# A two-block transformer kernel on one Trainium2 core: the last blocks of rows turned on VectorE and moved by DMA, not turned by TensorE

## The chip, the cores and the metric

The kernel runs on one core of one Trainium2 chip, in one launch. The metric is device time in microseconds (us) of that core. The engines are TensorE (PE, and PEld for its weight loads), VectorE (DVE), ScalarE (ACT), GpSimd (POOL) and SyncE (SP); all but VectorE and TensorE also issue DMAs. A trailing q (SPq, POOLq) is an engine's sequencer.

## The reference

One transformer block of each of two kinds, over 256 rows of width 2048, all in float32. Cut to the matrix products that matter:

```python
# first block
h = rmsnorm(x, attn_norm_g);  proj = h @ w_in          # c_q, c_kv, k_rope, u_pool, gates
q = (rmsnorm(c_q, q_a_norm_g) @ w_q_b);  kv = (rmsnorm(c_kv, kv_a_norm_g) @ w_kv_b)
y_attn = causal_block_attention(q, k, v) @ w_attn_o;   y_pool = pooled @ w_pool_o
mixed = g_pool * y_pool + g_attn * y_attn
x = x + mixed @ w_out
h2 = rmsnorm(x, ffn_norm_g)
x = x + (silu(h2 @ w_ffn_gate) * (h2 @ w_ffn_up)) @ w_ffn_down      # D_FF 5632
# second block
h = rms_norm(x, g_mix);  proj = h @ w_in_2             # q, k, v, u, v_sg, gates
merged = sigmoid(gate_a) * (o @ w_oa) + sigmoid(gate_b) * (s @ w_ob)
x = x + merged @ w_out_2
h2 = rms_norm(x, g_ff);  x = x + square(relu(h2 @ w_ff1)) @ w_ff2   # D_FF_2 8192
```

`o` is a stick-breaking attention and `s` a spatial gating unit. Each product's left operand has to stand in SBUF with its 2048 columns on the partitions, that is, turned.

## The kernel before, in words

**Products.** Each float32 product is three products of a reduced float32 kind: the left operand is kept as `lhs_hi` and its remainder `lhs_lo` (for 4 to 8 chunks of 128: `low_hi`, `low_lo`), each weight as `w_hi` and `w_lo`. SyncE loads 1 MB of weights at a time into `raw` (four slots), ScalarE copies them to `w_hi` (`hi`, L592), VectorE subtracts to get `w_lo` (`lo`, L1109). The unit is a granule: two chunks of 128 reduction rows by 512 output columns, for 256 rows of x, so twelve products (L1803, L1806, L1810). A panel is 512 output columns; a full one has eight granules in four groups. In ffn_last, panels 2 to 9 are short, with two granules each. The copies run four granules ahead of TensorE, and the loads three to four groups ahead (SyncE waits for `lo_ready`).

**Stages.** The stages follow in the order of `PLAN`: in, pool, heads_first, heads, heads_last, attn_o, out, ffn_first, ffn (nine turns of a loop), ffn_last, in2, gates2, mix2, out2, ffn2_first, ffn2 (fourteen turns), ffn2_last.

**Stage changes.** Between two stages the rows that a stage leaves (in `mix`, or in `xres` times a gain) become the left operand of the next, in four blocks of 512 columns. Each block can be written as soon as TensorE is done with that part of the old operand, and TensorE waits for it (`lhs_ready`) ahead of the group that reads it. There are two ways to turn a block:
- on TensorE: `pieces` transposes it in eight parts of 128x128 into PSUM (L1831, tile `aux`), ScalarE copies them to `lhs_hi` (L624), VectorE subtracts to get `lhs_lo` (L1146);
- in squares: VectorE turns all 32x32 squares in place (`flip_rows`, L1163) into `turn_x`, GpSimd issues sixteen DMAs of 32 KB that put the squares in their places in `turn_t` (`move_rows`, L551), ScalarE copies (`moved_block`, L657) and VectorE subtracts (`moved_block`, L1170). There are two buffers, so block n waits for block n - 2.

At attn_o to out, out to ffn_first, mix2 to out2 and out2 to ffn2_first (the four inner changes; functions `bridge`) the first three blocks go in squares and the fourth by TensorE, in the middle of the next stage's first panel (`gemm_after`, behind its second group). The fourth can only be started when the old stage's last panel is done. At ffn_last to in2 all four blocks go by TensorE. The two blocks of the low-rank rows (`cq_rows`, `ckv_rows`) are turned by TensorE in heads_first (`turn_low`, sixteen transposes).

**What sets the order.** Every engine's program is written out by hand, and each engine runs its own in order. Engines wait on semaphores; an instruction that waits holds up all behind it on its engine. GpSimd's and SyncE's DMAs are issued in their program's order too.

Of the kernel before, what the change touches and what calls it, by code (L numbers as in the profile page):

```python
# [38 lines left out]
P = 128  # L39
TOK = 2  # L40
# [127 lines left out]
def two_blocks(nc, x, positions, attn_norm_g, w_in, b_gate, q_a_norm_g, w_q_b, kv_a_norm_g, w_kv_b,  # L168
# [151 lines left out]
    rows_ready = sem("rows_ready")  # L320
# [7 lines left out]
    low_rows = sem("low_rows")  # L328
    low_turned = sem("low_turned")
# [26 lines left out]
    row_moved = [sem(f"row_moved{i}") for i in range(2)]  # L356
    flipped = sem("flipped")
# [31 lines left out]
    with block:  # L389

        @block.sync
        def _(sp):
# [11 lines left out]

            w1, w2 = w_in[0], w_in_2[0]
# [39 lines left out]
            for p in range(4):  # L445
                load(At("out"), p, w_out[0], p * N)
            at = At("ffn_first")
            load(at, 0, w_ffn_gate[0], 0)
            load(at, 1, w_ffn_up[0], 0)
# [14 lines left out]
            for p in range(10):  # L464
                load(At("in2"), p, w2, starts[p // 2] + p % 2 * N)
# [11 lines left out]
            for p in range(4):  # L477
                load(At("out2"), p, w_out_2[0], p * N)
# [25 lines left out]
        def _(pool):  # L504
# [20 lines left out]
            pool.wait_ge(low_turned, 4)  # L525
# [17 lines left out]
            def move_rows(n):  # L543
# [12 lines left out]
            for n in range(6):  # L556
                move_rows(n)
# [5 lines left out]
            with pool.Fori(1, NB1) as b:  # L563
                move(b)
            pool.wait_ge(side_go, 3)
# [9 lines left out]
            for n in range(6, 12):  # L575
                move_rows(n)
# [5 lines left out]
        def _(act):  # L582
# [172 lines left out]
            def turned_low():  # L755

                for q in range(4):
                    act.wait_ge(low_turned, q + 1)
                    c0, t = 4 * (q // 2), q % 2
                    nc.scalar.activation(low_hi[:, c0:c0 + 4, t * P:(t + 1) * P],  # L760
                                         aux[:, q, :].rearrange("p (c t) -> p c t", c=4),
                                         ACT.Copy).then_inc(low_hi_ready, 1)
# [54 lines left out]
            def sub(at, p, u, has_last, last=False):  # L817
# [5 lines left out]
                if has_last:  # L823
                    attend_b(u)
                else:
                    turned_low()
# [97 lines left out]
            hi(at, 6, 4, 8)  # L924
            squares_of(0, at, 6)
            pieces(3, 0)
            hi(at, 6, 8, 10)
            squares_of(1, at, 7)
            pieces(3, 1)
            hi(at, 6, 10, 12)  # L930
            squares_of(2, at, 8)
            pieces(3, 2)
            hi(nxt, 0, 4, 6)
            squares_of(3, at, 9)
            pieces(3, 3)
            hi(nxt, 0, 6, 8)
# [162 lines left out]
        def _(dve):  # L1099
# [34 lines left out]
            def gained(b):  # L1134
# [3 lines left out]
                                gain[:, c].unsqueeze(1).broadcast_to([P, TOK, N]), ALU.mult  # L1138
                                ).then_inc(rows_ready, 2)

            def pieces(n_hi, kq):

                for p in (2 * kq, 2 * kq + 1):
                    dst = slice(p % 2 * P, (p % 2 + 1) * P)
                    dve.wait_ge(lhs_hi_ready, n_hi + p + 1)
                    v.tensor_tensor(lhs_lo[:, 4 * kq:4 * kq + 4, dst],  # L1146
                                    aux[:, p % 4, :].rearrange("p (c t) -> p c t", c=4),
                                    lhs_hi[:, 4 * kq:4 * kq + 4, dst].bitcast(F32),
                                    ALU.subtract).then_inc(lhs_ready, 1)
# [23 lines left out]
            def bridge(n_hi, n, at, p, nxt, last_rows, between=None):  # L1173
# [10 lines left out]
                lo(nxt, 0, 4, 6)  # L1184
                pieces(n_hi, 3)
                lo(nxt, 0, 6, 8)
# [82 lines left out]
            dve.sem_inc(rows_ready, 8)  # L1269
# [53 lines left out]
            dve.sem_inc(low_rows, 1)  # L1323
# [10 lines left out]
            def turned_low():  # L1334
                for q in range(4):
                    dve.wait_ge(low_hi_ready, 8 + q + 1)
                    c0, t = 4 * (q // 2), q % 2
# [896 lines left out]
```

## Time and profile before

| | us |
|---|---|
| median of 3 runs | 2652.7 (2651.62 to 2652.74) |
| profiled execution | 2651.66 |
| its span, first to last instruction | 2650.0 |
| TensorE busy, 11949 products | 2643.5 |
| VectorE busy | 1662.7 |
| ScalarE busy | 1311.6 |
| GpSimd busy | 379.0 |

TensorE is busy all the time, so its row is the schedule: what is put on it lengthens the span, and so does what it waits for. The other engines' idle time is the slack in which they keep ahead. The granted clock of TensorE was full throughout in the profile, and the DMA engines moved 200 GB/s on average. In rows in order of time, an entry is the start, the duration of the run of like instructions, engine and line, operation, output from inputs, count, and in brackets the idle time ahead with what ended it. Products overlap, so a row's duration is a little longer than the distance to the next.

### The profile page before, as it was taken

Reading aid. Unit: us, or ns where it says so; the run is one execution under the profiler, and the core shown is the slowest. Engines: PE = TensorE matmul, PEld = TensorE weight load, DVE = VectorE, ACT = ScalarE, POOL = GpSimd, SP = SyncE. Lnnn points to the kernel's source line nnn. Section 1 sums busy time; section 2 is a strip of 40 time slices with the busy share of each in tenths; the row PEclk is TensorE's granted clock in tenths of the full one; section 3 lists DMA queues with packets and bytes.
Section 4 is the critical chain, followed back from the end, with each engine's and each line's share of the span. In section 5 each row is a group of like instructions: output and inputs, shape, how many; then the busy total and the mean of one; then the engine's idle time right before and its main releaser. Section 6 shows DMA issues by size and latency. Waiting matters only on the chain.

```text
span 2650.0 us, 33467 instructions
## 1 busy us (share of the span) xinstructions
PE 2643.5 (100%) x11949; PEld 2202.1 (83%) x11949; DVE 1662.7 (63%) x1671; ACT 1311.6 (49%) x1501; POOL 379.0 (14%) x767
## 2 busy tenths in 40 slices
PE   9999999999999999999999999999999999999999
PEld 8888888888888888888888888888888888888887
DVE  6556777666565665665576645556666666666666
ACT  5446666445444444444454547774454444444443
POOL 1000000222111111101103220003222121212121
PEclk9999999999999999999999999999999999999999
DMA  8555544666665666666667665456666666666664
GB/s 278 182 185 180 174 155 162 214 213 216 223 198 199 201 203 205 199 197 201 203 214 215 207 206 175 174 191 212 209 209 207 207 210 198 206 201 211 203 208 151
DMA packets 278041, 529.96 MB, mean 200 GB/s; under 512 B 20032, under 2 KB 26608, under 8 KB 277584
## 3 DMA queue, kind: packets, MB, share of 16 engines
q1 hardware_dynamic: 251600, 493.91, 56.1%
q0 software_dynamic: 26192, 35.01, 4.9%
q8 instruction: 46, 0.75, 0.1%
q14 instruction: 27, 0.22, 0.0%
q10 hardware_dynamic: 176, 0.07, 0.0%
HBM read 502.69 MB, written 2.10 MB: 190 GB/s over the span
## 4 chain that ended last, share of the span: by engine, by line
PE 99%; DVE 1%; DVEq 0%; DMA 0%; ACT 0%; issue 0%; ACTq 0%
PE pair L1810 27%; PE pair L1803 27%; PE pair L1806 27%; PE aux L1806 4%; PE aux L1810 4%; PE aux L1803 4%; PE aux L1831 1%; PE aux L1991 0%; PE aux L1988 0%; PE pair L1892 0%; PE pair L1899 0%; PE pair L1896 0%; PE aux L1950 0%; PE aux L2006 0%; PE aux L2123 0%; DMA act_t<-in_attn_norm_g 0%
## 5 line engine op out<-in xcount | busy, mean ns | idle before, releaser
L1109 DVE TENSOR_TENSOR w_lo<-raw,w_hi 128x1024 fp32r<-128x1024 f32 x944 | 1133.7, 1211 | 816.9 <-ACT w_hi L592 807.5
L592 ACT ACTIVATE w_hi<-raw 128x1024 fp32r<-128x1024 f32 (+2 forms) x942 | 983.3, 1051 | 1188.5 <-PE pair L1810 991.7
L1803 PE MATMUL pair<-w_hi,lhs_hi 128*128 128x512 f32 x2176 | 587.5, 392 | 0.0
L1810 PE MATMUL pair<-w_lo,lhs_hi 128*128 128x512 f32 x2176 | 582.4, 390 | 0.5 <-DVE w_lo L1109 0.5
L1806 PE MATMUL pair<-w_hi,lhs_lo 128*128 128x512 f32 x2176 | 582.4, 390 | 0.0
L1810 PEld LDWEIGHTS pair<-w_lo,lhs_hi 128*128 128x128 f32 x2176 | 408.5, 188 | 86.0 <-DVE w_lo L1109 0.9
L1806 PEld LDWEIGHTS pair<-w_hi,lhs_lo 128*128 128x128 f32 x2176 | 408.6, 188 | 85.5
L1803 PEld LDWEIGHTS pair<-w_hi,lhs_hi 128*128 128x128 f32 x2176 | 405.9, 188 | 81.8
L540 POOL DMA_DIRECT2D arena<-arena x544 | 265.7, 497 | 1276.3 <-DVE arena L1522 1044.6
L1803 PE MATMUL pair<-w_hi,low_hi 128*128 128x512 f32 (+1 forms) x1048 | 278.7, 388 | 0.0
L1806 PE MATMUL pair<-w_hi,low_lo 128*128 128x512 f32 (+1 forms) x1048 | 277.2, 386 | 0.0
L1810 PE MATMUL pair<-w_lo,low_hi 128*128 128x512 f32 (+1 forms) x1048 | 276.9, 386 | 0.0
L1806 PEld LDWEIGHTS pair<-w_hi,low_lo 128*128 128x128 f32 x1048 | 196.4, 188 | 38.5
L1810 PEld LDWEIGHTS pair<-w_lo,low_hi 128*128 128x128 f32 x1048 | 196.1, 188 | 38.4
L1803 PEld LDWEIGHTS pair<-w_hi,low_hi 128*128 128x128 f32 x1048 | 195.1, 188 | 38.2
L1456 DVE TENSOR_TENSOR xres<-xres,pair 128x1024 f32<-128x1024 f32 x115 | 139.7, 1215 | 1.9 <-PE pair L1810 1.9
L1810 PE MATMUL aux<-w_lo,lhs_hi 128*128 128x512 f32 x480 | 128.4, 389 | 0.0
L1806 PE MATMUL aux<-w_hi,lhs_lo 128*128 128x512 f32 x480 | 128.4, 389 | 0.0
L1803 PE MATMUL aux<-w_hi,lhs_hi 128*128 128x512 f32 x480 | 128.4, 389 | 0.0
L551 POOL DMA_DIRECT2D arena<-arena x192 | 93.8, 497 | 213.9 <-DVE arena L1163 143.9
L1810 PEld LDWEIGHTS aux<-w_lo,lhs_hi 128*128 128x128 f32 x480 | 90.1, 188 | 18.7
L1806 PEld LDWEIGHTS aux<-w_hi,lhs_lo 128*128 128x128 f32 x480 | 90.1, 188 | 18.7
(236 smaller groups left out, 1193.2 us busy)
## 6 DMA issues: line engine op xcount, KB each, us to landing
raw<-in_w_ff SPq DMA_DIRECT2D x128, 1024.0 KB, 5.1
raw<-in_w_in SPq DMA_DIRECT2D x118, 1024.0 KB, 5.1
raw<-in_w_ffn_gate SPq DMA_DIRECT2D x44, 1024.0 KB, 5.1
raw<-in_w_ffn_up SPq DMA_DIRECT2D x44, 1024.0 KB, 5.0
raw<-in_w_ffn_down SPq DMA_DIRECT2D x44, 1024.0 KB, 5.0
raw<-in_w_out SPq DMA_DIRECT2D x32, 1024.0 KB, 5.3
arena<-arena POOLq DMA_DIRECT2D x736, 32.0 KB, 3.9
raw<-in_w_attn_o SPq DMA_DIRECT2D x16, 1024.0 KB, 5.1
```

The lines of the kernel that those rows point to most:

```text
L540: pool.dma_start(dst[f * 32:(f + 1) * 32, a], src[a * 32:(a + 1) * 32, f]).then_inc(moved, 16)
L551: pool.dma_start(turn_t[n % 2][f * 32:(f + 1) * 32, a], turn_x[n % 2][a * 32:(a + 1) * 32, f]).then_inc(row_moved[n % 2], 16)
L592: nc.scalar.activation(w_hi[:, at.slot(p, k), :, 0:width], raw[:, at.raw_slot(p, k), 2 * h:2 * h + 2, 0:width], ACT.Copy).then_inc(hi_read ...
L1109: v.tensor_tensor(w_lo[:, at.slot(p, k), :, 0:n], raw[:, at.raw_slot(p, k), 2 * h:2 * h + 2, 0:n], w_hi[:, at.slot(p, k), :, 0:n].bitcast( ...
L1456: v.tensor_tensor(xs, xs, ps, ALU.add)
L1803: nc.tensor.matmul(ps[:, t, 0:n], hi_t[:, ch, tok], w_hi[:, s, c, 0:n], start=start and k == 0 and c == 0, stop=False)
L1806: nc.tensor.matmul(ps[:, t, 0:n], lo_t[:, ch, tok], w_hi[:, s, c, 0:n], start=False, stop=False)
L1810: mm = nc.tensor.matmul(ps[:, t, 0:n], hi_t[:, ch, tok], w_lo[:, s, c, 0:n], start=False, stop=stop and 2 * k + c == kch - 1)
L1831: return nc.tensor.transpose(dst, src, ident[0:src.shape[0], :])
```

## The change

All transposes of rows by TensorE at the stage changes are taken out, and so are those of the low-rank rows.
- The fourth block of the four inner changes is turned in squares, with all sixteen moves issued by GpSimd. VectorE's turn stands behind the block's last addition or gain; the copy and the subtraction stand between the splits of granules 6 and 7 of the next stage's first panel.
- At ffn_last to in2 all four blocks go in squares, and eight of each block's sixteen moves are issued by GpSimd and eight by SyncE, between its weight loads (`HALVED`, `move_half`).
- The low-rank rows are turned at the start of the pool stage by two turns on VectorE and 32 moves from GpSimd, and copied and subtracted in heads_first.
- The semaphores follow; the blocks are numbered four to a change.

The core of the diff (on SyncE some loads of out, ffn_first and out2 are also written as two calls, which issue the same DMAs):

```diff
+    low_x = [part(0, 4, 4 * TOK, 32), part(2048, 4, 4 * TOK, 32)]
+    low_t = [part(1024, 4, 4 * TOK, 32), part(3072, 4, 4 * TOK, 32)]
-    BLOCKS = [(r, f, kq) for r, f in ((1, 2), (2, 3), (4, 6), (5, 7)) for kq in range(3)]
+    BLOCKS = [(r, f, kq) for r, f in ((1, 2), (2, 3), (3, 4), (4, 6), (5, 7)) for kq in range(4)]
+    HALVED = [r == 3 for r, f, kq in BLOCKS]
...
@@ SyncE
+            def move_half(n):
+                sp.wait_ge(row_flipped, n + 1)
+                r, f, kq = BLOCKS[n - 2]
+                sp.wait_ge(lhs_ready, 8 * f + 2 * kq + 2)
+                for f in range(2, 4):
+                    for a in range(4):
+                        sp.dma_start(turn_t[n % 2][f * 32:(f + 1) * 32, a],
+                                     turn_x[n % 2][a * 32:(a + 1) * 32, f]).then_inc(half_moved[n % 2], 16)
...
-            for p in range(10):
-                load(At("in2"), p, w2, starts[p // 2] + p % 2 * N)
+            at = At("in2")
+            load(at, 0, w2, 0, groups=[0])
+            for b in range(4):
+                load(at, (b + 1) // 4, w2, (b + 1) // 4 * N, groups=[(b + 1) % 4])
+                move_half(8 + b)
+            load(at, 1, w2, N, groups=[1, 2, 3])
...
@@ GpSimd
-            pool.wait_ge(low_turned, 4)
+            pool.wait_ge(low_flipped, 2)
+            for b in range(2):
+                for f in range(4):
+                    for a in range(4):
+                        pool.dma_start(low_t[b][f * 32:(f + 1) * 32, a], low_x[b][a * 32:(a + 1) * 32, f]
+                                       ).then_inc(low_moved, 16)
...
-                for f in range(4):
+                for f in range(2 if HALVED[n] else 4):
...
@@ ScalarE, bridge
-                hi(nxt, 0, 4, 6)
-                pieces(r, 3, at.gran(p, 8) + SPLIT)
-                hi(nxt, 0, 6, 8)
+                hi(nxt, 0, 4, 7)
+                moved_block(n + 3, 3, at.gran(p, 8) + SPLIT)
+                hi(nxt, 0, 7, 8)
...
@@ VectorE, bridge
                 last_rows()
-                lo(nxt, 0, 4, 6)
-                pieces(n_hi, 3)
-                lo(nxt, 0, 6, 8)
+                flip_rows(n + 3)
+                lo(nxt, 0, 4, 7)
+                moved_block(n_hi, n + 3, 3)
+                lo(nxt, 0, 7, 8)
...
@@ VectorE, ffn_last
             for j in range(4):
-                lo(at, 6 + j, 4, 6)
+                lo(at, 6 + j, 4, 5)
                 add_x(at, 6 + j, j * N)
                 gained(j)
-                if j:
-                    pieces(28, j - 1)
-            lo(nxt, 0, 4, 6)
-            pieces(28, 3)
-            lo(nxt, 0, 6, 8)
+                flip_rows(8 + j)
+                if j >= 2:
+                    moved_block(28, 6 + j, j - 2)
+                lo(at, 6 + j, 5, 6)
+            lo(nxt, 0, 4, 5)
+            moved_block(28, 10, 2)
+            lo(nxt, 0, 5, 7)
+            moved_block(28, 11, 3)
+            lo(nxt, 0, 7, 8)
...
@@ TensorE
-            def gemm_after(at, f, left, c0=0, r=None, ps=None):
+            def gemm_after(at, f, left, c0=0, ps=None):
                 for g in range(4):
                     pe.wait_ge(lhs_ready, 8 * f + 2 * g + 2)
                     gemm(at, 0, left, c0, [g], ps)
-                    if g == 1:
-                        pieces(r, f, 3)
...
-                else:
-                    turn_low()
...
             for j in range(4):
                 gemm(at, 6 + j, low, 4)
-                if j:
-                    pieces(3, 4, j - 1)
```

**Order at out to ffn_first, VectorE, before.** L1170 is the subtraction of a block that came in squares, L1456 the last panel's addition to `xres`, L1137 the gain, L1109 a split of weights, L1146 the subtraction of a block turned by TensorE.

```order
L1109 TENSOR_TENSOR w_lo<-raw,w_hi 128x1024 x4
L1170 TENSOR_TENSOR lhs_lo<-arena,lhs_hi 128x1024
L1456 TENSOR_TENSOR xres<-xres,pair 128x2x512
L1137 TENSOR_TENSOR mix<-xres,arena 128x2x512
L1109 TENSOR_TENSOR w_lo<-raw,w_hi 128x1024 x2
L1146 TENSOR_TENSOR lhs_lo<-aux,lhs_hi 128x4x128 x2
L1109 TENSOR_TENSOR w_lo<-raw,w_hi 128x1024 x6
```

The same place after the change, by the changed kernel's lines: L1190 is the subtraction, L1476 the addition, L1165 the gain, L1183 the turn in squares, L1137 a split of weights.

```order
L1137 TENSOR_TENSOR w_lo<-raw,w_hi 128x1024 x4
L1190 TENSOR_TENSOR lhs_lo<-arena,lhs_hi 128x1024
L1476 TENSOR_TENSOR xres<-xres,pair 128x2x512
L1165 TENSOR_TENSOR mix<-xres,arena 128x2x512
L1183 STREAM_TRANSPOSE arena<-mix 128x8x4x32
L1137 TENSOR_TENSOR w_lo<-raw,w_hi 128x1024 x3
L1190 TENSOR_TENSOR lhs_lo<-arena,lhs_hi 128x1024
L1137 TENSOR_TENSOR w_lo<-raw,w_hi 128x1024 x5
```

The turn comes in behind the gain, and the fourth block's subtraction moves from behind two splits of the next stage to behind three.

**Order at ffn_last to in2, VectorE, before**, from the addition of panel 7 on.

```order
L1456 TENSOR_TENSOR xres<-xres,pair 128x2x512
L1137 TENSOR_TENSOR mix<-xres,arena 128x2x512
L1146 TENSOR_TENSOR lhs_lo<-aux,lhs_hi 128x4x128 x2
L1109 TENSOR_TENSOR w_lo<-raw,w_hi 128x1024 x2
L1456 TENSOR_TENSOR xres<-xres,pair 128x2x512
L1137 TENSOR_TENSOR mix<-xres,arena 128x2x512
L1146 TENSOR_TENSOR lhs_lo<-aux,lhs_hi 128x4x128 x2
```

After the change, from the addition of panel 7 to the turn of panel 9.

```order
L1476 TENSOR_TENSOR xres<-xres,pair 128x2x512
L1165 TENSOR_TENSOR mix<-xres,arena 128x2x512
L1183 STREAM_TRANSPOSE arena<-mix 128x8x4x32
L1137 TENSOR_TENSOR w_lo<-raw,w_hi 128x1024 x2
L1476 TENSOR_TENSOR xres<-xres,pair 128x2x512
L1165 TENSOR_TENSOR mix<-xres,arena 128x2x512
L1183 STREAM_TRANSPOSE arena<-mix 128x8x4x32
L1190 TENSOR_TENSOR lhs_lo<-arena,lhs_hi 128x1024
L1137 TENSOR_TENSOR w_lo<-raw,w_hi 128x1024 x2
L1476 TENSOR_TENSOR xres<-xres,pair 128x2x512
L1165 TENSOR_TENSOR mix<-xres,arena 128x2x512
L1183 STREAM_TRANSPOSE arena<-mix 128x8x4x32
```

Per panel there is one turn more, and block 0's subtraction, which stood behind the gain of panel 7, now stands behind the turn of panel 8.

## Rows read from the trace of the kernel before

**Rows 1.** The page: busy engines (us, share, instructions); shares of the last chain.
```profile
PE 2643.5 (100%) x11949; PEld 2202.1 (83%) x11949; DVE 1662.7 (63%) x1671; ACT 1311.6 (49%) x1501; POOL 379.0 (14%) x767
PE 99%; DVE 1%; DVEq 0%; DMA 0%; ACT 0%; issue 0%; ACTq 0%
```

**Rows 2.** Costliest groups: busy, mean ns | idle before, its releaser.
```profile
L1109 DVE TENSOR_TENSOR w_lo<-raw,w_hi 128x1024 fp32r<-128x1024 f32 x944 | 1133.7, 1211 | 816.9 <-ACT w_hi L592 807.5
```

**Rows 3.** TensorE reading mix: ns min/median/max, first and last start.
```profile
L1831 PE MATMUL aux<-con,mix x80: 270/273/274, 172.1 to 1961.2; 128*128 128x128 f32 x80
```

**Rows 4.** Order of time, out to ffn_first: start us, us, engine, line.
```profile
638.62 1.07 PE L1803 MATMUL pair<-w_hi,lhs_hi 128*128 128x512 f32 x4
641.12 1.22 DVE L1170 TENSOR_TENSOR lhs_lo<-arena,lhs_hi 128x1024 fp32r<-128x1024 f32 x1
642.26 1.22 DVE L1456 TENSOR_TENSOR xres<-xres,pair 128x1024 f32<-128x1024 f32 x1
643.59 1.22 DVE L1137 TENSOR_TENSOR mix<-xres,arena 128x1024 f32<-128x1024 f32 x1
644.73 2.35 DVE L1109 TENSOR_TENSOR w_lo<-raw,w_hi 128x1024 fp32r<-128x1024 f32 x2
649.51 1.04 PE L1831 MATMUL aux<-con,mix 128*128 128x128 f32 x8
650.30 1.17 PE L1803 MATMUL pair<-w_hi,lhs_hi 128*128 128x512 f32 x4
```

**Rows 5.** Order of time, TensorE in heads_first.
```profile
172.08 1.91 PE L1831 MATMUL aux<-con,mix 128*128 128x128 f32 x16
173.74 1.17 PE L1803 MATMUL pair<-w_hi,lhs_hi 128*128 128x512 f32 x4
```

**Rows 6.** Order of time, the first block of stage out.
```profile
577.25 1.23 DVE L1137 TENSOR_TENSOR mix<-xres,arena 128x1024 f32<-128x1024 f32 x1 [0.19 <-issue]
578.57 1.25 DVE L1163 STREAM_TRANSPOSE arena<-mix 128x1024 f32<-128x1024 f32 x1
579.74 2.32 DVE L1109 TENSOR_TENSOR w_lo<-raw,w_hi 128x1024 fp32r<-128x1024 f32 x2
580.11 7.81 POOL L551 DMA_DIRECT2D arena<-arena  x16 [32.84 <-DVE arena L1163]
```

**Rows 7.** Order of time, moves in in2 that ScalarE waited for.
```profile
1570.39 7.81 POOL L540 DMA_DIRECT2D arena<-arena  x16 [14.15 <-DVE arena L1522]
1581.30 1.06 ACT L1006 ACTIVATE act_t<-arena 128x1024 f32<-128x1024 f32 x1 [3.04 <-DMA arena<-arena]
```

**Rows 8.** DMA issues from 1573.5, 1577.5, 609.1, 647.0: count, size, landing us.
```profile
arena<-arena POOLq DMA_DIRECT2D x2, 32.0 KB, 1.9
arena<-arena POOLq DMA_DIRECT2D x2, 32.0 KB, 3.6
arena<-arena POOLq DMA_DIRECT2D x2, 32.0 KB, 5.2
raw<-in_w_ffn_up SPq DMA_DIRECT2D x1, 1024.0 KB, 5.0
```

**Rows 9.** Windows: busy us (count) by engine, PEclk, DMA share, GB/s.
```profile
649.00:651.40 2.40, 2.40 (x16) 2.06 (x16) 0.62 (x2) 1.25 (x3) 0.00 (x0) 1.00 0.98 370
651.60:654.60 3.00, 3.00 (x15) 2.47 (x14) 2.83 (x3) 2.86 (x6) 0.00 (x0) 1.00 0.00 1
```

**Rows 10.** Order of time, attn_o to out.
```profile
550.69 1.07 PE L1803 MATMUL pair<-w_hi,lhs_hi 128*128 128x512 f32 x4
557.00 2.36 DVE L1109 TENSOR_TENSOR w_lo<-raw,w_hi 128x1024 fp32r<-128x1024 f32 x2
```

**Rows 11.** Order of time, TensorE at ffn_last, panel 7.
```profile
1341.31 1.07 PE L1803 MATMUL pair<-w_hi,low_hi 128*128 128x512 f32 x4
```

**Rows 12.** Filler products at the start, and window 0 to 3 us.
```profile
L1873 PE MATMUL pair<-arena x30: 275/276/581, 1.2 to 8.3; 128*128 128x128 f32 x30
0.00:3.00 3.00, 1.80 (x8) 1.81 (x9) 0.71 (x3) 1.12 (x1) 0.20 (x4) 1.00 0.33 69
```

More of the change, by code:

```diff
@@ L356, in two_blocks @@
     row_moved = [sem(f"row_moved{i}") for i in range(2)]
+    half_moved = [sem(f"half_moved{i}") for i in range(2)]
     flipped = sem("flipped")
@@ L444, in _ @@
                 load(at, 2 + p, w_attn_o[0], p * N)
-            for p in range(4):
-                load(At("out"), p, w_out[0], p * N)
+            at = At("out")
+            load(at, 0, w_out[0], 0)
+            load(at, 1, w_out[0], N, groups=[0])
+            load(at, 1, w_out[0], N, groups=[1, 2, 3])
+            for p in range(2, 4):
+                load(at, p, w_out[0], p * N)
             at = At("ffn_first")
             load(at, 0, w_ffn_gate[0], 0)
-            load(at, 1, w_ffn_up[0], 0)
+            load(at, 1, w_ffn_up[0], 0, groups=[0])
+            load(at, 1, w_ffn_up[0], 0, groups=[1, 2, 3])
             def ffn_block(at, i):
@@ L463, in _ @@
             starts = (0, SB, COL_VS, COL_U, 2 * SB)
-            for p in range(10):
-                load(At("in2"), p, w2, starts[p // 2] + p % 2 * N)
+            at = At("in2")
[4 more added lines that the diff above has]
+            load(at, 1, w2, N, groups=[1, 2, 3])
+            for p in range(2, 10):
+                load(at, p, w2, starts[p // 2] + p % 2 * N)
             with sp.Fori(0, 2) as i:
@@ L476, in _ @@
                 load(At("mix2", i), 1, w_oa_2[0], i * N)
-            for p in range(4):
-                load(At("out2"), p, w_out_2[0], p * N)
+            at = At("out2")
+            load(at, 0, w_out_2[0], 0)
+            load(at, 1, w_out_2[0], N, groups=[0])
+            load(at, 1, w_out_2[0], N, groups=[1, 2, 3])
+            for p in range(2, 4):
+                load(at, p, w_out_2[0], p * N)
             load(At("ffn2_first"), 0, w_ff1_2[0], 0)
@@ L555, in _ @@
             to_all(gain, ffn_norm_g[0], "gain")
-            for n in range(6):
+            for n in range(8):
                 move_rows(n)
@@ L564, in _ @@
                 move(b)
+            for n in range(8, 12):
+                move_rows(n)
             pool.wait_ge(side_go, 3)
@@ L574, in _ @@
             to_all(gain, g_ff_2[0], "gain")
-            for n in range(6, 12):
+            for n in range(12, 20):
                 move_rows(n)
@@ L752, in _, with moved_low @@
                     hi(at, p, 4, 8)
[L755 to L762, printed above, removed]
+            def moved_low():
+                act.wait_ge(low_moved, 512)
+                for b in range(2):
+                    nc.scalar.activation(hid_rows(low_hi, 4 * b), low_t[b].rearrange("p a n i -> p n a i"),
+                                         ACT.Copy).then_inc(low_hi_ready, 2)
             def attend_a(u):
@@ L1137, in gained @@
                 v.tensor_tensor(mix[:, :, c], xres[:, :, c],
[L1138 to L1149, printed above, removed]
+                                gain[:, c].unsqueeze(1).broadcast_to([P, TOK, N]), ALU.mult)
+                dve.drain()
             def refill(n_hi, kq):
@@ L1322, in _ @@
             low_norm(4, 2, 2, gain_ckv, ckv_rows)
-            dve.sem_inc(low_rows, 1)
+            for b, rows in enumerate((cq_rows, ckv_rows)):
+                v.transpose(low_x[b].rearrange("p f n i -> p n f i"),
+                            rows.rearrange("p t (c d) -> p c t d", c=4)).then_inc(low_flipped, 1)
             with dve.Fori(0, 2) as i:
@@ L1508, in out_panels @@
                 bridge(n_hi, n, at, 3, nxt, last_block)
-            out_panels(At("out"), At("ffn_first"), 20, 3, 1)
+            out_panels(At("out"), At("ffn_first"), 20, 4, 1)
             def hid_turn(b, c0=0):
@@ L1959, in _ @@
                         gemm(At("pool", i), p, low, groups=[g])
-            def turn_low():
-                pe.wait_ge(low_rows, 1)
-                for q in range(4):
-                    rows = cq_rows if q < 2 else ckv_rows
-                    for c in range(4):
-                        ins = turn(aux[:, q, c * P:(c + 1) * P], rows[:, q % 2, c * P:(c + 1) * P])
-                    ins.then_inc(low_turned, 1)
             def turn_qk(u):
```

100 lines of the change are left out of this document (42 added, 58 removed).

## The prediction

> **What bounds the kernel now.** I read the busy times first, then the chain that ended last, then the waits, then the order of time at each place where one weight stage hands over to the next. TensorE is busy for 2643.5 of 2650.0 us and makes up 99% of the chain [rows 1]. The splitting of weights on VectorE, 1133.7 us, is the largest other group, and it waits for ScalarE and TensorE, not they for it [rows 2]. So two things change the time: TensorE instructions that go, and waits put in front of TensorE.
>
> One granule (twelve products of 512 columns) takes 2.72 us: from 638.62, the start of ffn_first, to 649.51 there are four, 10.89 us [rows 4]. A whole panel is eight of them, 21.76 us, one of the short panels of ffn_last two, 5.44 us.
>
> **What is removed.** 80 turns by TensorE go: the whole group that reads mix [rows 3]. Sixteen stand in heads_first, eight at each of the four inner changes (attn_o to out, out to ffn_first, mix2 to out2, out2 to ffn2_first), 32 between ffn_last and in2. Eight cost 650.30 - 649.51 = 0.79 us, and the four products behind them last 1.17 in place of 1.07 us: 0.89 in all [rows 4]. Sixteen cost 173.74 - 172.08 = 1.66, and the same 0.10 behind them: 1.76 [rows 5]. The sum is 8 x 0.89 + 1.76 = 8.9 us off TensorE, if nothing waits.
>
> **heads_first.** The two squares of the low-rank rows are turned at the start of the pool stage. VectorE gets two turns of 1.25 us there and GpSimd 32 moves of 7.81 / 16 = 0.49 us, 15.6 us [rows 6]. Between that and the use lie four panels of four granules and more, 43.5 us. I take no wait; GpSimd's memset and bias load behind them have the same slack. Gain 1.76.
>
> **The four inner changes.** This is the step that decides. In before, the fourth block was added, multiplied and turned on TensorE with time to spare. Now it goes through VectorE's turn, sixteen moves from GpSimd's queue, ScalarE's copy and VectorE's subtraction, and TensorE wants it at the fourth group of the next stage's first panel, six granules in: E + 16.32, where E is the start of that stage. At out to ffn_first, E = 638.62:
> - VectorE subtracts the third block from 641.12, adds the residual at 642.26, multiplies by the gain at 643.59, and goes on at 644.73, E + 6.1 [rows 4]. An earlier block shows the turn 1.32 us behind the gain, with the drain: E + 6.29. It lasts 1.25, and GpSimd starts 0.29 behind its end (580.11 against 578.57 + 1.25): E + 7.83 [rows 6].
> - Sixteen issues take 7.81 us, so the last starts 7.32 in: E + 15.15. This is the term that eats the time: the last square isn't asked for until 1.2 us before TensorE wants the whole block.
> - Landing of the last. With the DMA engines free, issues land in 1.9 us; while a 1 MB weight load runs, 3.6 and 5.2 us [rows 8]. In before a load issued at 647.0 to 647.5 lands after 5.0, and the engines carry 0.98 of their capacity from 649.0 to 651.4 and nothing from 651.6 to 654.6 [rows 8, 9]. It is released by VectorE's split of granule 5, which now comes one turn later, so the load's packets are through near 653.1. The last move is issued at 653.8, behind a small backlog. I take 2.2, next to the 1.9 of free engines: E + 17.35.
> - ScalarE's copy 1.06 [rows 7], about 0.2 to VectorE's start, subtraction 1.22 [rows 4], 0.1 to TensorE: E + 19.95.
>
> TensorE waits 19.95 - 16.32 = 3.6 us. Bounds: landing 1.9 gives 3.3, landing 5.2 gives 6.6. The only move in before that a reader waited for was read 10.91 us behind its first issue (1570.39 to 1581.30) against my 7.32 + 2.2 = 9.5; that gives 5.0 [rows 7]. There a load ran to the end, so I keep 3.6.
>
> The other three changes have the same distances; attn_o to out has E = 550.69, and VectorE is free for the turn at 557.00, E + 6.31 [rows 10]. Four waits: 14.4 us. Queued behind the waiting copy and subtraction are the split of granule 7 and of the next panel's first granules; ScalarE needs about 1.1 us for each (its copies of that size, rows 7) and VectorE 1.21 [rows 2], where TensorE takes 2.72, and granule 7 is wanted only 2.72 us after the wait ends, so nothing more is late. The gain is 4 x 0.89 = 3.6, the net +10.8.
>
> By the Trainium skill, page "DMA: Bandwidth & Descriptors", section "Anatomy of one DMA — SWDGE (gpsimd) path", a GpSimd DMA costs a fixed 2.0 us or so plus its bytes over about 436 GB/s; an estimate from that page is 2.1 us for 32 KB, and the sum would be 0.4 us lower over the four changes. This trace agrees on free engines and not under a load, where it shows 5.2.
>
> **ffn_last to in2.** All four blocks go by squares, eight moves on GpSimd and eight on SP, while short panels of 5.44 us run. GpSimd needs 3.9 us a block, so issue isn't the limit; VectorE is. From start to start of the next it takes per panel two splits (1.15 us each), the addition (1.33), the gain (1.32), the turn (1.17) and later a subtraction (1.14): about 7.3 us against 5.44 [rows 4, 6]. Panel 7 starts at 1341.31 [rows 11], and panel 6 can be added from 1341.6. From there I stack VectorE's instructions in the new order: block 0 is subtracted at about 1358.9, and in2 could start at 1341.31 + 3 x 5.44 = 1357.6. Wait 1.3. Block 1 is subtracted 7.3 later, TensorE wants it 5.44 later: 1.8 more. Block 2 follows in time (1370 against 1371.6), block 3 with about 1 us to spare. Waits 3.1 against 4 x 0.89 = 3.6 gained: net -0.5. Bounds: 0 if the stacking is loose by that much, 7 if each of blocks 2 and 3 lands as late as 5.2. SP's weight loads queue behind its moves, held up to the turn of each block; they are issued three to four groups ahead, some 16 us, and are held 3 us.
>
> **The sum.** -8.9 + 14.4 + 3.1 = +8.6 us. The profiled execution took 2651.66 us around its span of 2650.0, so 2660.3 like for like. The median of the runs shown is 1.0 higher, so 2661.3 is forecast.
>
> **Rivals.**
> - *The landing is slow after all.* Each last move lands in 3.6 us, as in the one move that was waited for [rows 7, 8]. Waits of 5.0: +5.6, 2666.9. At 5.2 with the queue in its way, 6.6 each: 2673. For it: it is the only wait for moves that these rows show. Against it: the idle stretch of rows 9. Chance 0.18.
> - *The clock falls.* At the very start the filler products last up to 581 ns where the median is 276: half speed, 1.2 for 2.4 GHz, though the profile's granted clock reads 1.00 there [rows 12]. TensorE had done nothing before. If each wait of 3.6 us ends in such a stretch of about the first product group's length, 14 products at up to twice their time, some 1.6 us are lost at each of four: 2667.7. Against it: in before TensorE never rests that long, so no row shows it. The Trainium skill, page "TensorE: Matmul & The Clock Gate", Part 1, says that the slow state is the default and that an idle TensorE returns to it. Chance 0.10.
> - *Blocks 2 and 3 are late at in2*, because GpSimd waits for the subtraction of the block two before: up to 2 us each, 2665. Chance 0.07.
> - *Faster.* The squares arrive before TensorE wants them, and only the 8.9 us less the 3.1 stay: 2646.9. The four waits would have to fall under (8.9 - 3.1) / 4 = 1.45 each for the kernel not to be slower; that is a chain 2.2 us shorter than I stack it. The rows leave no slack of that size: the sixteen issues alone fill all but 1.2 us. Chance 0.05 to the full, and 0.03 for a result between.
> - The forecast itself: 0.57.
>
> What a measurement of this kernel can tell from no change is about 0.2%, 5.3 us: 2647.4 to 2658.0. The forecast lies 3.3 above that; in one of ten of its cases the waits are short enough to fall inside. With the cases between that makes 0.09 for the same; faster keeps 0.05; slower 0.86. The range holds the forecast's own bounds (3.3 us a wait and no wait at in2, 2657) with the slow landing and the clock above: 2656 to 2672.
>
> **What would show it.** Right: at each inner change TensorE stands 3 to 5 us between the second granule of the third group and the fourth group, ended by VectorE's subtraction of lhs_lo, with ScalarE's copy ended by a DMA; about 1.3 and 1.8 us at the start of in2 and its second group, ended by VectorE without idle time ahead of it; no wait in heads_first; no turns of mix by TensorE. Wrong: ScalarE's copy starts without a wait for the moves; a gap at another granule; long products behind a gap; VectorE idle before the subtraction of block 0 in in2.

## The result and the profile after

| | before | after |
|---|---|---|
| median | 2652.16 (4 runs, 2651.56 to 2652.74) | 2674.85 (4 runs, 2673.51 to 2676.58) |
| profiled execution | 2651.66 | 2673.51 |
| its span | 2650.0 | 2671.8 |

The ratio is 1.0086, interval [1.0074, 1.0098]. The changed kernel is slower by 22.7 us. The forecast was 2661.3, within 2656 to 2672: the sign was right, the size was not. (It was built on the median of three runs of before, 2652.7; with the fourth it is 2652.16.) Like for like, the profiled executions differ by +21.85 us where the sum said +8.6.

The page of the changed kernel, busy engines and the shares of the chain that ended last, to set beside [rows 1]:

```profile
PE 2645.2 (99%) x11869; PEld 2199.6 (82%) x11869; DVE 1672.0 (63%) x1671; ACT 1311.3 (49%) x1491; POOL 441.6 (17%) x895
PE 94%; DVE 2%; POOL 1%; DMA 1%; DVEq 1%; ACT 1%; issue 1%; ACTq 0%; POOLq 0%
```

Eighty TensorE instructions are gone, and yet TensorE is busy for 1.7 us more. Fewer instructions in more busy time: some of them must have become slower. And the chain now leaves TensorE for VectorE, GpSimd and the DMAs.

The waits of TensorE, and of ScalarE from attn_o to ffn_first, in the changed kernel (for what: us in total, times, longest):

```profile
PE pair L1825 <- DVE lhs_lo L1190: 20.3, 6, 4.6
PE pair L1825 <- DVE low_lo L1533: 0.8, 1, 0.8
ACT lhs_hi L685 <- DMA arena<-arena: 17.8, 2, 9.1
```

Six waits for a block's subtraction: the four inner changes and two at in2. In the changed kernel L1825, L1828 and L1832 are the three products of a granule (L1803, L1806 and L1810 before), L1190 is the subtraction, L1183 the turn, L685 ScalarE's copy of a moved block, L590 the moves.

Order of time at attn_o to out, from E = 549.63, which answers to [rows 4] and [rows 10]:

```profile
549.63 1.07 PE L1825 MATMUL pair<-w_hi,lhs_hi 128*128 128x512 f32 x4
555.90 1.25 DVE L1183 STREAM_TRANSPOSE arena<-mix 128x1024 f32<-128x1024 f32 x1
557.43 7.82 POOL L590 DMA_DIRECT2D arena<-arena  x16 [11.44 <-DVE arena L1183]
568.23 1.06 ACT L685 ACTIVATE lhs_hi<-arena 128x1024 fp32r<-128x1024 f32 x1 [9.12 <-DMA arena<-arena]
569.38 1.23 DVE L1190 TENSOR_TENSOR lhs_lo<-arena,lhs_hi 128x1024 fp32r<-128x1024 f32 x1 [8.87 <-ACT lhs_hi L685]
570.67 2.08 PE L1825 MATMUL pair<-w_hi,lhs_hi 128*128 128x512 f32 x4 [4.56 <-DVE lhs_lo L1190]
572.54 1.91 PE L1828 MATMUL pair<-w_hi,lhs_lo 128*128 128x512 f32 x4
574.24 1.85 PE L1832 MATMUL pair<-w_lo,lhs_hi 128*128 128x512 f32 x4
575.93 1.09 PE L1825 MATMUL pair<-w_hi,lhs_hi 128*128 128x512 f32 x4
```

The turn starts at E + 6.27 and the moves at E + 7.80; the forecast had 6.29 and 7.83. From there it is off twice. ScalarE's copy starts at E + 18.60 instead of 17.35, so TensorE starts its fourth group at E + 21.04, 4.7 us late instead of 3.6. And the first twelve products behind the wait take 5.26 us from start to start (575.93 - 570.67) where a granule took 2.72 [rows 4]: 2.5 us more.

The windows around it, changed kernel (busy us and count of PE, PEld, DVE, ACT, POOL; granted clock; DMA share; GB/s), to set beside [rows 9]:

```profile
560.00:566.00 6.00, 6.00 (x27) 4.71 (x26) 0.52 (x1) 0.00 (x0) 5.25 (x11) 1.00 0.84 244
566.00:568.00 2.00, 0.11 (x1) 0.00 (x0) 0.00 (x0) 0.00 (x0) 0.00 (x0) 1.00 0.01 1
570.00:576.00 6.00, 5.33 (x13) 4.24 (x14) 4.01 (x4) 2.12 (x3) 0.00 (x0) 0.51 0.50 164
576.00:580.00 4.00, 4.00 (x19) 3.29 (x18) 1.23 (x1) 2.11 (x2) 0.00 (x0) 1.00 0.74 278
```

The granted clock reads 0.51 from 570 to 576, that is 1.2 of 2.4 GHz, and 1.00 from 576 on. What TensorE did before it fell: nothing, for 4.56 us. The first row is the other miss: while the moves are issued, the DMA engines are at 0.84 of their capacity, not free. By queue (q1 is SyncE's load, q0 are GpSimd's moves; packets, MB, share of the 16 engines), from 563 to 564 and from 564 to 565:

```profile
q1 hardware_dynamic: 192, 0.39, 100.0%
q0 software_dynamic: 12, 0.02, 4.4%
```

```profile
q0 software_dynamic: 214, 0.23, 101.2%
q1 hardware_dynamic: 23, 0.02, 7.0%
```

The load has the engines nearly to itself until 564, and the moves issued beside it get 4%. Then they are all carried at once, and the last move, issued at 564.75, comes behind them.

At the other three changes the same picture stands. The rows of the changed kernel at out to ffn_first, mix2 to out2 and out2 to ffn2_first:

```profile
664.60 2.07 PE L1825 MATMUL pair<-w_hi,lhs_hi 128*128 128x512 f32 x4 [4.15 <-DVE lhs_lo L1190]
666.47 1.82 PE L1828 MATMUL pair<-w_hi,lhs_lo 128*128 128x512 f32 x4
668.12 1.09 PE L1832 MATMUL pair<-w_lo,lhs_hi 128*128 128x512 f32 x4
...
1892.67 1.48 PE L1825 MATMUL pair<-w_hi,lhs_hi 128*128 128x512 f32 x4 [4.34 <-DVE lhs_lo L1190]
1893.95 1.91 PE L1828 MATMUL pair<-w_hi,lhs_lo 128*128 128x512 f32 x4
...
1986.11 2.08 PE L1825 MATMUL pair<-w_hi,lhs_hi 128*128 128x512 f32 x4 [4.46 <-DVE lhs_lo L1190]
1987.98 1.57 PE L1828 MATMUL pair<-w_hi,lhs_lo 128*128 128x512 f32 x4
```

Waits: 4.56 + 4.15 + 4.34 + 4.46 = 17.5 us; counted against E + 16.32 the fourth groups start 4.7, 4.3, 4.5 and 4.6 late, 18.1 in all. Slow products (what each four take beyond 0.907 us from start to start, until the pace is back): 2.6 + 1.7 + 1.8 + 1.5 = 7.6 us. (The expectations below have 7.5 for it.)

At in2 the changed kernel's TensorE waits nearly as forecast, 1.3 and 1.5 us, and the products behind keep their pace within 0.2 us, as they did behind the turns in before [rows 4]:

```profile
1369.57 1.21 PE L1825 MATMUL pair<-w_hi,lhs_hi 128*128 128x512 f32 x4 [1.30 <-DVE lhs_lo L1190]
1376.81 1.20 PE L1825 MATMUL pair<-w_hi,lhs_hi 128*128 128x512 f32 x4 [1.47 <-DVE lhs_lo L1190]
```

### The profile page after: what moved, and what is told of

It is laid out like the page before. It is cut to its first block, busy times and chain, and to the rows that moved or that the text cites. A ratio compares the mean times of both kernels' runs of the same rounds, so it can differ in the third digit from the quotient of the medians.

```text
span 2671.8 us, 33485 instructions
## 1 busy us (share of the span) xinstructions
PE 2645.2 (99%) x11869; PEld 2199.6 (82%) x11869; DVE 1672.0 (63%) x1671; ACT 1311.3 (49%) x1491; POOL 441.6 (17%) x895
## 4 chain that ended last, share of the span: by engine, by line
PE 94%; DVE 2%; POOL 1%; DMA 1%; DVEq 1%; ACT 1%; issue 1%; ACTq 0%; POOLq 0%
PE pair L1825 26%; PE pair L1828 26%; PE pair L1832 26%; PE aux L1825 4%; PE aux L1832 4%; PE aux L1828 4%; POOL arena L590 1%; PE aux L1853 1%; DMA arena<-arena 1%; DVE w_lo L1137 0%; PE aux L1989 0%; PE aux L1986 0%; DVE lhs_lo L1190 0%; DVE arena L1183 0%; PE pair L1900 0%
## 5 line engine op out<-in xcount | busy, mean ns | idle before, releaser
L1137 DVE TENSOR_TENSOR w_lo<-raw,w_hi 128x1024 fp32r<-128x1024 f32 x944 | 1132.0, 1210 | 807.2 <-ACT w_hi L633 800.2
L1825 PE MATMUL pair<-w_hi,lhs_hi 128*128 128x512 f32 x2176 | 590.2, 393 | 20.3 <-DVE lhs_lo L1190 20.3
L1828 PE MATMUL pair<-w_hi,lhs_lo 128*128 128x512 f32 x2176 | 585.0, 391 | 0.0
L1832 PE MATMUL pair<-w_lo,lhs_hi 128*128 128x512 f32 x2176 | 583.4, 390 | 0.5 <-DVE w_lo L1137 0.5
L1825 PEld LDWEIGHTS pair<-w_hi,lhs_hi 128*128 128x128 f32 x2176 | 407.5, 189 | 105.4 <-DVE lhs_lo L1190 22.8
L1828 PEld LDWEIGHTS pair<-w_hi,lhs_lo 128*128 128x128 f32 x2176 | 410.7, 189 | 86.4
L1832 PEld LDWEIGHTS pair<-w_lo,lhs_hi 128*128 128x128 f32 x2176 | 409.7, 188 | 86.6 <-DVE w_lo L1137 0.9
L579 POOL DMA_DIRECT2D arena<-arena x544 | 265.7, 497 | 1259.1 <-DVE arena L1540 1046.5
L1825 PE MATMUL pair<-w_hi,low_hi 128*128 128x512 f32 (+1 forms) x1048 | 278.5, 387 | 0.8 <-DVE low_lo L1533 0.8
L1828 PE MATMUL pair<-w_hi,low_lo 128*128 128x512 f32 (+1 forms) x1048 | 277.0, 386 | 0.0
L1832 PE MATMUL pair<-w_lo,low_hi 128*128 128x512 f32 (+1 forms) x1048 | 276.7, 386 | 0.0
L1828 PEld LDWEIGHTS pair<-w_hi,low_lo 128*128 128x128 f32 x1048 | 196.4, 188 | 38.5
L1832 PEld LDWEIGHTS pair<-w_lo,low_hi 128*128 128x128 f32 x1048 | 196.0, 188 | 38.4
L1825 PEld LDWEIGHTS pair<-w_hi,low_hi 128*128 128x128 f32 x1048 | 195.1, 188 | 39.5 <-issue 1.2
L590 POOL DMA_DIRECT2D arena<-arena x288 | 140.7, 497 | 260.4 <-DVE arena L1183 183.5
L1476 DVE TENSOR_TENSOR xres<-xres,pair 128x1024 f32<-128x1024 f32 x115 | 139.5, 1213 | 2.2 <-PE pair L1832 2.2
L1825 PE MATMUL aux<-w_hi,lhs_hi 128*128 128x512 f32 x480 | 128.3, 389 | 0.0
L1828 PE MATMUL aux<-w_hi,lhs_lo 128*128 128x512 f32 x480 | 128.3, 389 | 0.0
L1832 PE MATMUL aux<-w_lo,lhs_hi 128*128 128x512 f32 x480 | 128.3, 389 | 0.0
L1825 PEld LDWEIGHTS aux<-w_hi,lhs_hi 128*128 128x128 f32 x480 | 90.1, 188 | 18.7
L1828 PEld LDWEIGHTS aux<-w_hi,lhs_lo 128*128 128x128 f32 x480 | 90.1, 188 | 18.7
```

The lines of the kernel that those rows point to most:

```text
L579: pool.dma_start(dst[f * 32:(f + 1) * 32, a], src[a * 32:(a + 1) * 32, f]).then_inc(moved, 16)
L590: pool.dma_start(turn_t[n % 2][f * 32:(f + 1) * 32, a], turn_x[n % 2][a * 32:(a + 1) * 32, f]).then_inc(row_moved[n % 2], 16)
L1137: v.tensor_tensor(w_lo[:, at.slot(p, k), :, 0:n], raw[:, at.raw_slot(p, k), 2 * h:2 * h + 2, 0:n], w_hi[:, at.slot(p, k), :, 0:n].bitcast( ...
L1476: v.tensor_tensor(xs, xs, ps, ALU.add)
L1825: nc.tensor.matmul(ps[:, t, 0:n], hi_t[:, ch, tok], w_hi[:, s, c, 0:n], start=start and k == 0 and c == 0, stop=False)
L1828: nc.tensor.matmul(ps[:, t, 0:n], lo_t[:, ch, tok], w_hi[:, s, c, 0:n], start=False, stop=False)
```

## The experiments

All are the changed kernel with one thing altered, in two of them with two. Times are medians; each ratio is to the kernel before on the same chip. Sums over the four inner changes are of TensorE's waits in the profile and of slow products, as above; the kernel before has 0 and, behind its turns, 0.4.

| version | median us | ratio, interval | waits | slow |
|---|---|---|---|---|
| changed kernel | 2674.85 | 1.0086 [1.0074, 1.0098] | 17.5 | 7.6 |
| fourth blocks back on TensorE | 2650.51 | 0.9993 [0.9983, 1.0003] | 0 | 0.4 |
| 36 fillers in each wait | 2680.71 | 1.0110 [1.0093, 1.0127] | 0 | 0.4 |
| 18 fillers | 2667.05 | 1.0058 [1.0041, 1.0074] | 1.5 | 0.5 |
| load held back | 2665.83 | 1.0052 [1.0035, 1.0069] | 11.8 | 6.7 |
| load held back, 12 fillers | 2661.77 | 1.0037 [1.0022, 1.0051] | 1.4 | 0.6 |
| moves on two queues | 2648.23 | 0.9984 [0.9975, 0.9994] | 0.6 | 0.8 |
| the same, VectorE reordered at in2 | 2647.16 | 0.9981 [0.9972, 0.9991] | 0.4 | 0.8 |

### The fourth blocks back on TensorE

The four inner changes are as in before; heads_first and in2 stay changed.

```diff
-BLOCKS = [(r, f, kq) for r, f in ((1, 2), (2, 3), (3, 4), (4, 6), (5, 7)) for kq in range(4)]
+BLOCKS = [(r, f, kq) for r, f in ((1, 2), (2, 3), (3, 4), (4, 6), (5, 7)) for kq in range(4 if r == 3 else 3)]
... (ScalarE's copy and VectorE's subtraction back to before's; blocks numbered anew)
@@ TensorE, gemm_after, behind the second group
+    pe.wait_ge(rows_ready, last + 1)
+    for t in range(TOK):
+        for c in range(4):
+            ins = turn(aux[:, 2 + t, c * P:(c + 1) * P], mix[:, t, (12 + c) * P:(13 + c) * P])
+        ins.then_inc(turned, 1)
```

> The changed kernel with the fourth block of the four inner changes turned by TensorE again; in2 and the low-rank rows stay as changed. My theory (the loss sits in the waits at the four inner changes, 18.1 us, and in the slow products behind them, 7.5 us): all of that goes, the turns come back at 4 x 0.89 = 3.6 us, and what is left is -1.8 (heads_first) and -3.6 + 3.3 at in2: 2650 us, 2 below the kernel before. Rival (the moves and SyncE's blocks at in2 cost more than the gaps there show): 2655 or more.

Measured: 2650.51 us, and no wait at any inner change. The inner changes carry all of the loss, 2674.85 - 2650.51 = 24.3 us. The rest of the change agrees with what the sum gave it: 1.76 + 3.56 gained against 3.1 waited is 2.2 us off 2652.2, so 2650.0. It is small, though: the interval of this version holds 1, so the run by itself does not tell this gain from none.

### Thirty-six fillers ahead of the fourth group

```diff
 for g in range(4):
+    if g == 3:
+        for _ in range(fill):
+            nc.tensor.matmul(aux[:, 0, 0:P], ident, ident, start=True, stop=True)
...
-            gemm_after(at, 2, wide)
+            gemm_after(at, 2, wide, fill=36)
... (and the same for the operands 3, 6 and 7)
```

> The changed kernel with 36 filler products (128x128, some 0.11 us each, 4 us in all) on TensorE ahead of the wait for the fourth block, at each inner change. Theory A (the products behind each wait are slow because TensorE's clock fell to half while it rested): the waits stay in sum, the slow products go, -7.5 us: 2667.4. Theory B (they are slow because ScalarE and VectorE then make up three granules each at once and all read the same memory): nothing changes, 2674.9, and the product group behind the wait still lasts about 2 us. The granted clock behind the wait, 0.51 in the changed kernel, reads 1.00 by A.

Measured: 2680.71 us, neither. I had priced a filler at half of what it takes. Order of time of this version at attn_o to out:

```profile
565.50 8.20 PE L1860 MATMUL aux<-con 128*128 128x128 f32 x72
573.46 1.17 PE L1825 MATMUL pair<-w_hi,lhs_hi 128*128 128x512 f32 x4
574.46 1.07 PE L1828 MATMUL pair<-w_hi,lhs_lo 128*128 128x512 f32 x4
```

Each float32 filler is two instructions in the trace; 36 of them take 8.2 us, 0.228 each, and TensorE does not wait but fills past the block's arrival. The four fillings cost 7.96 each against E + 16.32, 31.8 us, in place of 18.1 + 7.6. One thing it does show: behind 8 us of fillers the products take 1.07, at full pace. As a test of the theory it failed, since another cost came in its place, so it was run again with the right number.

### Eighteen fillers

The same edit, with 18.

> The changed kernel with 18 filler products (128 columns each, into a bank that nothing reads) on TensorE ahead of the fourth group at each of the four inner changes. The run with 36 of them showed 0.228 us for each: 18 take 4.1 us and fit inside the waits of 4.15 to 4.56 us, where 36 took 8.2 us and ran past them. Theory A (the wait is set by the arrival of the block, and the slow products behind it by TensorE's rest): the fourth group starts when it did in the changed kernel, the products behind it take full time, the profile shows waits of 0.1 to 0.5 us there, and the 7.5 us of slow products go: 2667.4. Rival B (the slow products come from something else that happens then, such as the weights' arrival or the transfers beside them): the waits are filled, the products stay slow, 2674.9.

Measured: 2667.05 us against 2667.4 by theory A. Order of time of this version at attn_o to out, and the window behind:

```profile
565.01 4.18 PE L1860 MATMUL aux<-con 128*128 128x128 f32 x36
569.22 1.20 PE L1825 MATMUL pair<-w_hi,lhs_hi 128*128 128x512 f32 x4
...
569.00:575.00 6.00, 5.96 (x27) 4.80 (x26) 4.80 (x5) 2.75 (x3) 0.00 (x0) 1.00 0.59 198
```

The fourth group still starts late, for the block comes no sooner, but the clock reads 1.00 and the products have their pace. This version takes 7.8 us less than the changed kernel, whose trace has 7.6 of slow products. So the slow products are the price of TensorE's rest and of nothing else that happens there: the weights, the moves and the copies are the same in both. (The fourth groups start 4.2, 4.3, 4.6 and 5.3 us late here, 18.4 in all for 18.1. The last is late by more than its fillers last, and a wait of 1.15 us is left there: VectorE's turn of that block starts at E + 7.2, where it starts at E + 6.3 at attn_o to out.)

### The load held back

SyncE issues the weight load that runs beside the fourth block's moves, of groups 2 and 3 of the next panel, only when those moves have landed.

```diff
-load(at, 1, w_out[0], N, groups=[1, 2, 3])
+load(at, 1, w_out[0], N, groups=[1])
+sp.wait_ge(row_moved[1], pool_moves(3))
+load(at, 1, w_out[0], N, groups=[2, 3])
```

and the same at the other three changes.

> The changed kernel with the one weight load that overlaps the fourth block's moves held on SyncE until they have landed (groups 2 and 3 of the next panel). Theory L (the last moves land after 3.2 and not 2 us because that load fills the DMA engines): last landing near 2.0, each wait 1.2 shorter, 4.8 us less, and perhaps a shorter slow stretch behind: 2668 to 2670. Theory Q (the depth of GpSimd's own queue of sixteen does it): landings stay at 3 us and the time at 2674.9. If the held load itself comes too late, a new gap some 8 granules on, and slower.

Measured: 2665.83 us, 9.0 less. Landing of the last three moves at attn_o to out, the changed kernel (issued from 564.2 to 565.0) and this version (564.7 to 565.5), with its windows:

```profile
arena<-arena POOLq DMA_DIRECT2D x3, 32.0 KB, 3.2
```

```profile
arena<-arena POOLq DMA_DIRECT2D x3, 32.0 KB, 1.7
560.00:566.00 6.00, 6.00 (x28) 4.96 (x27) 1.04 (x1) 0.00 (x0) 5.77 (x12) 1.00 0.27 70
570.00:573.00 3.00, 3.00 (x9) 2.33 (x8) 2.82 (x3) 0.93 (x1) 0.00 (x0) 0.55 0.84 276
569.47 1.41 PE L1833 MATMUL pair<-w_hi,lhs_hi 128*128 128x512 f32 x4 [2.84 <-DVE lhs_lo L1198]
570.68 1.91 PE L1836 MATMUL pair<-w_hi,lhs_lo 128*128 128x512 f32 x4
```

With the DMA engines at 0.27 and not 0.84, the last moves land in 1.7 us instead of 3.2, and the wait is 2.84 instead of 4.56. Waits: 17.5 to 11.8; slow products 7.6 to 6.7. That is 6.6 less, and with 1.2 more at the first turn of ffn2 and at the kernel's start it makes the 5.4 us between the two profiled executions (2673.51 to 2668.10); the other 3.6 of the 9.0 between the medians no trace shows, for the profiled execution was the slowest of this version's four. TensorE waits for no weights because of the held load. A rest of 2.84 to 3.26 us is followed by slow products all the same, 1.5 to 1.8 us a change, at a granted clock of 0.55 behind the first: the clock's part hardly falls with the wait.

### The load held back, and twelve fillers

Both edits, with 12 fillers (2.7 us). It takes away both things that the forecast had left out.

> The version whose second weight load of the stage is held until the moves have landed, with 12 filler products (2.7 us) in each of its four waits of 2.84 to 3.26 us. It has both causes taken away that the forecast left out: a landing beside a load, and TensorE's clock after a rest. Theory A with L: the version with the loads held, 2665.8, less its 6.7 us of slow products: 2659.1, which is within 2.5 us of the forecast. If the landing did not grow shorter through the held load but through something else, or the slow products are not TensorE's rest, it stays at 2665.8.

Measured: 2661.77 us, 2.7 more than 2659.1. Between the profiled executions it is 6.5 us, 2668.10 to 2661.61, close to the theory's 6.7; between the medians, taken on two chips, only 4.1, for the reason given above. The trace has both effects gone: waits of 0.17, 0.42, 0.62 and 0.21 us behind the fillers, and products at full pace. This is close to the kernel that the forecast had in mind, and it stands 0.5 us from the 2661.3 forecast. That it comes so near is partly luck: its fourth groups start 3.0 to 3.5 us late, 12.8 in all for 14.4, since the last moves land in 1.7 and not 2.2, and what the sum lacks elsewhere (the last terms of the new sum below) makes up for it.

### The moves on two queues

SyncE issues eight of the sixteen moves at the inner changes too, as at in2.

```diff
-HALVED = [r == 3 for r, f, kq in BLOCKS]
+HALVED = [r == 3 or kq == 3 for r, f, kq in BLOCKS]
...
@@ SyncE, at each of out, ffn_first and out2 behind the load of group 0
+    move_half(3)                       # 7, 15; 19 behind ffn2_first's load
```

> The changed kernel with eight of the fourth block's sixteen moves issued by SyncE at the inner changes too, as at in2. Theory I (the serial issue on one queue, 7.8 us, is what makes the block late): SyncE needs 5.0 us for eight, so the last move goes out 2.8 to 3.1 us earlier, the waits shrink from 4.5 to 1.5 us, and after so short a rest the products behind run at full clock: 4 x 3.0 + 7.5 = 19.5 us less, 2655.4. If the wait shrinks and the slow products stay: 2663. If landing, not issue, set the time: 2670 or more.

Measured: 2648.23 us, 7.2 below 2655.4. Order of time of this version at attn_o to out, and its windows:

```profile
557.79 5.63 SPq L421 DMA_DIRECT2D arena<-arena  x8
558.05 3.92 POOL L594 DMA_DIRECT2D arena<-arena  x8 [11.43 <-DVE arena L1187]
563.46 7.60 SPq L410 DMA_DIRECT2D raw<-in_w_out  x4
564.87 1.06 ACT L689 ACTIVATE lhs_hi<-arena 128x1024 fp32r<-128x1024 f32 x1 [5.14 <-DMA arena<-arena]
567.31 1.20 PE L1829 MATMUL pair<-w_hi,lhs_hi 128*128 128x512 f32 x4 [0.58 <-DVE lhs_lo L1194]
560.00:566.00 6.00, 6.00 (x28) 4.99 (x27) 1.14 (x2) 1.13 (x2) 1.97 (x5) 1.00 0.39 106
567.00:573.00 6.00, 5.69 (x25) 4.70 (x26) 4.89 (x5) 2.83 (x3) 0.00 (x0) 1.00 1.05 388
```

On the slower of the two queues the issue is over at E + 13.2 (E = 566.57 - 16.32 = 550.25 here), where GpSimd alone needed until E + 15.6, and the load stands behind the moves on SyncE's queue (563.46), so nothing is in their way: the split also does what the held load did. ScalarE's copy starts at E + 14.6 instead of 18.6. What is left is one wait of 0.58 us; the other three changes have none in the view, and the clock stays up. So one edit takes away issue time, slow landing and slow products together, 18.1 + 7.6 us by the trace of the changed kernel less about 1.5 that stay, and with them the wait at the first turn of ffn2, 0.8 us in the changed kernel. The profiled executions differ by 24.9 and the medians by 26.6. How much of it is the split and how much the load behind it, this run does not divide. This version beats both kernels: 0.9984 of before.

### VectorE reordered at in2

In addition, the subtraction of blocks 0 and 1 goes ahead of the gain and the turn of blocks 2 and 3.

```diff
 add_x(at, 6 + j, j * N)
+if j >= 2:
+    moved_block(28, 6 + j, j - 2)
 gained(j)
 flip_rows(8 + j)
-if j >= 2:
-    moved_block(28, 6 + j, j - 2)
```

> The version with eight of the sixteen moves of each inner fourth block on SP's queue, and in addition VectorE's subtraction of blocks 0 and 1 ahead of in2 placed before the multiplication by the gain and the turn of blocks 2 and 3 instead of behind them. Theory V (the waits of 1.0 and 1.5 us at in2 are VectorE's order of work): the first goes, the second shrinks to about 0.3, and because blocks 2 and 3 are turned 1.2 us later the third and fourth group wait up to 0.4 and 1.1; in sum 1.8 in place of 2.5 to 2.8 us, 2647.2 against 2648.2. Rival W (the waits are the landing of the moves or ScalarE's copy): they stay as they are and the later turns add to them, 2649 to 2650.

Measured: 2647.16 us against 2647.2. TensorE's waits for a subtraction over the whole kernel, the version on two queues and then this one:

```profile
PE pair L1829 <- DVE lhs_lo L1194: 3.1, 3, 1.5
```

```profile
PE pair L1829 <- DVE lhs_lo L1194: 1.6, 3, 0.8
```

The wait at in2's first group is gone, the second is 0.45, and a new one of 0.77 stands at the fourth. The in2 waits were VectorE's order, as forecast. The intervals of the two versions overlap, so the 1.1 us between them rest on the traces. It is the best version run: 0.9981 of before, 5.1 us.

## Why the prediction was wrong in size

**What held.** The turns removed and their price, -8.9; the fourth blocks as the step that decides; the chain on VectorE and GpSimd up to the moves within 0.03 us (0.2 at mix2 to out2); sixteen issues of 0.49 us; ScalarE's copy, the subtraction, and the place of the wait; in2's groups 1.3 and 1.8 late by the forecast and 1.5 and 1.8 in the trace (waits of 1.30 and 1.47). Slower was given 0.86.

**Step that failed 1: "Landing of the last ... I take 2.2".** It was 3.2 us (3.0, 2.8 and 3.4 at the other changes) and ScalarE read the block 3.5 behind the last issue. The forecast let the load's packets be through at E + 14.5, before the last move, and there it was right: they are through soon after 564.0, E + 14.4. What it made small is the backlog: the moves issued beside the load had got under a tenth of the engines (4% from 563 to 564) and were carried at full capacity from 564 to 565, ahead of the last one. The held load shows it: 1.7. The term of the four waits, 14.4, came out as 18.1: +3.7. The bound of 3.6 was written down from [rows 8], and the value taken was the one next to free engines, though the load was known to run beside most of the moves.

**Step that failed 2: "The clock falls", chance 0.10, kept out of the sum.** It fell at all four, for 7.6 us in all, 1.9 each; the rival's price of 1.6 was near. The argument against it, that no row of before shows so long a rest, was no argument: the change makes the rest, so before cannot show it. [Rows 12] did show what products cost behind an idle TensorE, twice their time, although the granted clock reads 1.00 in that window. The Trainium skill, page "TensorE: Matmul & The Clock Gate", Part 1, which the prediction names, says that an idle TensorE returns to the slow state. The changed kernel's trace agrees: behind the rest of 4.56 us the granted clock is 0.51. The prediction's own list of signs of being wrong has it too, "long products behind a gap". Eighteen fillers that keep TensorE busy through the wait bring 7.8 us back.

**How the range was built.** The slow landing (2666.9) and the clock (2667.7) stood as alternatives. They are not: a longer wait is, if anything, a surer rest. Together, by the prediction's own prices, waits of 5.0 and four times 1.6, they give 2666.9 + 6.4 = 2673.3, within 1.6 us of what was measured and outside the range. That it comes so near is luck in part: the fourth groups were 4.5 late on average and not 5.0, the slow products cost 1.9 and not 1.6, and three smaller terms are lacking.

**The new sum.** 8.6 + 3.7 (landing) + 7.6 (clock) + 0.2 (in2) + 1.0 (the first turn of ffn2 starts late; its wait of 0.8 was not forecast) + 0.7 = 21.8, against 21.85 between the profiled executions. The last 0.7 is no part of the change: the kernel's first eight transposes and the fillers behind them ran at about half pace for longer in this execution than in that of before, so the first product of the first granule starts 0.7 later. Changed kernel, then before:

```profile
5.64 1.97 PE L1853 MATMUL aux<-con,xres 128*128 128x128 f32 x8
10.05 1.16 PE L1900 MATMUL pair<-w_hi,lhs_hi 128*128 128x512 f32 x4
```

```profile
5.67 1.09 PE L1831 MATMUL aux<-con,xres 128*128 128x128 f32 x8
9.36 1.16 PE L1892 MATMUL pair<-w_hi,lhs_hi 128*128 128x512 f32 x4 [0.81 <-issue]
```

The executions of the other versions have either time for the eight, 1.97 or 1.09. Why ffn2's first block is late was not tried: GpSimd starts its moves at 2001.80, 3.3 us behind the end of VectorE's turn (0.6 in before), with idle time that the view puts down to issue. The version on two queues shows nearly the same gap without a wait, so the gap by itself isn't the reason; the cause stays open.

**The rival on the other side** needed waits under 1.45 us each. The changed kernel had 4.4; two queues have 0.58 at one change and none at three, and end below before by 4 us. The idea of the change was good, its issue on one queue was not.

## What to carry to other kernels

A long wait put in front of TensorE costs twice: the wait, and slow products behind it. Here a rest of 2.8 to 4.6 us cost 1.5 to 2.6 us more, nearly whatever its length, and one of 0.6 or 1.5 us cost 0.2 or less; nothing between was measured. A profile in which TensorE never rests can't show that price, so put it into the sum, and add such rivals up where they can come true together. Where many small DMAs stand just ahead of a deadline, count their issues first, divide them over queues, and place the large load behind them on the same queue. When a load does run beside them, ask not only when it ends but how many of them it has held back.

## What the runs showed of the hardware

- The last of sixteen small DMAs, issued just behind a 1 MB load's packets, landed in 3.2 us; with the load held back in 1.7. While the load ran (563 to 564) its queue had 100.0% of the engines and the small ones' 4.4%.
- SyncE takes 4.95 to 5.63 us to issue eight moves of 32 KB, GpSimd 3.92: for these, GpSimd is the faster queue, and the two side by side still beat it alone (7.82 for sixteen) by 2.2 to 2.9 us.
- With 4.56 us without work TensorE went on at a granted clock of 0.51 and was at 1.00 again some 5 us later; at the other three changes the pace was back 3.3 to 4.5 us after the first product. Fillers of 128 columns into an unused bank held the clock at 1.00; one in float32 costs 0.228 us, and too many cost more than the clock did (2680.71 against 2674.85).
